# The last expert's down products, scatter and sums moved into the gMLP block, with its down weights loaded by rows in two parts

## The reference

```python
def _expert_choice_ffn(x, norm_g, w_router, w_e_gate, w_e_up, w_e_down):
    ...
    gate, idx = lax.top_k(jnp.swapaxes(aff, 1, 2), cap)
    xg = xn[bidx, idx]
    h = (jax.nn.silu(jnp.einsum('becd,edf->becf', xg, w_e_gate))
         * jnp.einsum('becd,edf->becf', xg, w_e_up))
    yo = jnp.einsum('becf,efd->becd', h, w_e_down) * gate[..., None].astype(xg.dtype)
    return jnp.zeros((B, S, D), yo.dtype).at[bidx, idx].add(yo)

def gmlp_mixer(h, w_in, v_gain, w_sp, b_sp, w_out):
    uv = jax.nn.gelu(h @ w_in)
    u, v = jnp.split(uv, 2, axis=-1)
    v = layer_norm_gain(v, v_gain)
    ...
    return (u * z.reshape(B, S, D_GATE)) @ w_out
```

## Time and profile before

| | us |
|---|---|
| three runs | 1567.84, 1568.64, 1570.01 (median 1568.64) |
| the profiled execution | 1567.67 |
| its span, first to last instruction | 1565.6 |
| PE busy | 1333.9 (85%) |
| PE weight loads busy | 846.7 (54%) |
| DVE, ACT, POOL busy | 513.4, 483.1, 221.9 |
| mean granted TensorE clock | 0.942 of full |

### The profile page before, as it was taken

How to read it: one execution, slowest core, us unless ns; L and a number is a source line. 1 busy time by engine, 2 the same in 40 slices (tenths; PEclk the granted TensorE clock), 3 DMA queues, 4 the chain that set the end, 5 groups by cost and what they waited for, 6 DMA issues and landing times. The chain is left out here.

```text
span 1565.6 us, 18070 instructions
## 1 busy us (share of the span) xinstructions
PE 1333.9 (85%) x7114; PEld 846.7 (54%) x7114; DVE 513.4 (33%) x874; ACT 483.1 (31%) x739; POOL 221.9 (14%) x134
## 2 busy tenths in 40 slices
PE   7999999998766676766767677899999999999998
PEld 7778878633221221121212122777888777778886
DVE  5887768310000000000000000544333436643333
ACT  6656664310000000000000000635444367564442
POOL 0010000000000000000000000662232171123221
PEclk9999999999989988779998987999999999999999
DMA  7564437999999999999999999655556464365650
GB/s 243 173 173 116 119 126 285 391 428 428 430 430 430 430 429 430 430 430 430 430 429 430 429 430 422 238 161 182 189 171 204 142 200 138 99 198 178 197 165 27
DMA packets 123296, 446.81 MB, mean 285 GB/s; under 512 B 9193, under 2 KB 61801, under 8 KB 98673
## 3 DMA queue, kind: packets, MB, share of 16 engines
q1 hardware_dynamic: 121616, 445.30, 73.7%
q10 hardware_dynamic: 1632, 0.88, 0.2%
HBM read 445.10 MB, written 1.05 MB: 285 GB/s over the span
## 5 line engine op out<-in xcount | busy, mean ns | idle before, releaser
L1459 PE MATMUL ps<-sb_ring,sb_consts 128*32 128x384 f32 x2032 | 204.0, 539 | 120.0 <-DMA sb_ring<-w_e_up 98.0
L1459 PEld LDWEIGHTS ps<-sb_ring,sb_consts 128*32 128x32 f32 x2032 | 61.5, 116 | 260.2 <-DMA sb_ring<-w_e_up 144.4
L169 PE MATMUL ps<-net_whi,sb_xhi 128*128 128x512 f32 x480 | 190.0, 396 | 5.1 <-DVE sb_xlo L242 3.3
L1480 PE MATMUL ps<-sb_e_ring,sb_hT 128*32 128x512 f32 x576 | 191.9, 649 | 2.1 <-DMA sb_e_ring<-w_e_down 1.9
L171 PE MATMUL ps<-net_whi,sb_xlo 128*128 128x512 f32 x480 | 187.1, 390 | 0.0
L170 PE MATMUL ps<-net_wlo,sb_xhi 128*128 128x512 f32 x480 | 186.9, 389 | 0.0
L1480 PE MATMUL ps<-sb_ring,sb_hT 128*32 128x512 f32 x192 | 114.2, 758 | 54.4 <-DMA sb_e_ring<-w_e_down 53.6
L1871 ACT ACTIVATE net_whi<-sb_ring 128x2048 fp32r<-128x2048 f32 x64 | 122.3, 1914 | 64.0 <-PE ps L171 61.7
L1559 DVE TENSOR_TENSOR sb_sg<-ps,sb_sg 128x384 f32<-128x384 f32 x16 | 8.9, 557 | 365.3 <-PE ps L1459 365.3
L1884 POOL TENSOR_TENSOR net_wlo<-sb_ring,net_whi 128x2048 fp32r<-128x2048 f32 x20 | 92.2, 4610 | 215.3 <-ACT net_whi L1871 215.3
L1884 DVE TENSOR_TENSOR net_wlo<-sb_ring,net_whi 128x2048 fp32r<-128x2048 f32 x44 | 101.0, 2295 | 51.0 <-ACT net_whi L1871 51.0
(11 more groups left out here) (355 smaller groups left out, 1902.3 us busy)
## 6 DMA issues: line engine op xcount, KB each, us to landing
sb_ring<-w_e_up SPq DMA_DIRECT2D x64, 1536.0 KB, 37.7
sb_ring<-w_e_gate SPq DMA_DIRECT2D x63, 1536.0 KB, 37.0
sb_e_ring<-w_e_down SPq DMA_DIRECT2D x48, 1536.0 KB, 35.3
sb_ring<-ffn_w_gu SPq DMA_DIRECT2D x88, 512.0 KB, 4.6
sb_ring<-w_e_down SPq DMA_DIRECT2D x16, 1536.0 KB, 32.5
sb_ring<-ffn_w_down SPq DMA_DIRECT2D x22, 1024.0 KB, 4.9
sb_ring<-w_in SPq DMA_DIRECT2D x40, 512.0 KB, 3.6
sb_ring<-a_w_in SPq DMA_DIRECT2D x8, 1024.0 KB, 13.4
```

What stands on the lines that cost most here:

```text
L169: pe.matmul(out, hi, whi, start=start, stop=False)
L1459: mm = pe.matmul(ps[j * CAP:(j + 1) * CAP, GATE if i < 4 else UP, 0:FJ], xgs[:, k, :], rows[:, q * E_FF + j * FJ:q * E_FF + (j + 1) * FJ], ...
L1480: mm = pe.matmul(ps[j * CAP:(j + 1) * CAP, DOWN[h], :], hT[:, b, j * CAP:(j + 1) * CAP], expert_unit(m, NGU + j)[:, b * D + h * BANK:b * D ...
```

## The change

- The last expert leaves the loops. Its hidden part stays in the experts' block on PE, ACT and DVE. The transposes, the copy of `hT`, down products, scatter and the copies to `m.x` stand at the start of the gMLP block, the copies between the splits of the first granules.
- Its down weights come in two parts (`load_last_rows`): of each partition's three rows of 4 KB the first two, for all four groups, then the third. The products go by the same parts, all four groups side by side. Ahead of the first part PE does six 128x512 products whose result nothing reads, ahead of the second one.
- v0 is cut into four granules of two chunks (128 x 1024, half a MB) for two of four. The six granules that SP issues ahead are now v0 and v1.
- x is turned and split in halves of four chunks, each once its half of x is copied.
- Buffers that must outlive the experts' block move: two units form `m.mid`, which the mixer's stream and the attention use too, and `e_ring`, `hotgs`, `sg`, `hT` lie on the right side of the memory; gMLP's `ut`, `vt`, `tmp`, `wsp` and `gain` take expert units.

```diff
+def load_last_rows(sp, m, I, e, i):
+
+    b0, nb = ((0, FB - 1), (FB - 1, 1))[i]
+    src = I["w_e_down"][0, e, :, :].rearrange("(j p b) n -> p j (b n)", b=FB, p=P)[:, :, b0 * D:(b0 + nb) * D]
+    sp.dma_start(expert_unit(m, NGU)[:, b0 * D:(b0 + nb) * D], src[:, 0, :]).then_inc(m.e_landed[NGU + i], 16)
+    dst = m.e_ring[:, 0:3 * SLOT].rearrange("p (j n) -> p j n", j=3)[:, :, b0 * D:(b0 + nb) * D]
+    sp.dma_start(dst, src[:, 1:, :]).then_inc(m.e_landed[NGU + i], 16)
...
-            with sp.Fori(2, N_EXP) as e:
+            with sp.Fori(2, LAST) as e:
                 for i in range(NS):
                     load(e, i)
+            for i in range(NGU):
+                load(LAST, i)
+            sp.wait_ge(used, LAST * NS)
+            for i in range(2):
+                load_last_rows(sp, m, I, LAST, i)
             sp.wait_ge(used, (N_EXP - 1) * NS + RING)
             for g in range(st.slots):
                 st.load(sp, g)
...
-    for name, n0 in (("v0", D), ("v1", D + BANK), ("u0", 0), ("u1", BANK)):
+    at["v0"] = [st.add([(0, 2, BANK, chunks(I["a_w_in_2"][0], k, 2, D, BANK))], True) for k in range(0, DC, 2)]
+    for name, n0 in (("v1", D + BANK), ("u0", 0), ("u1", BANK)):
...
+            act.wait_ge(g_ps, 1)
+            act.activation(m.gs, ps[:, UP, 0:SEQ], ACT.Copy).then_inc(gs_ready, 1)
+            act.wait_ge(y_ps, 1)
+            act.activation(m.ysb[:, 0:BANK], ps[:, DOWN[0], :], ACT.Copy).then_inc(y_act, 1)
             st.split_hi(act, first)
-            norm_hi_act(act, m, use, NB, m.xhi, col(m, "gmlp"), xhi_ready, 0)
-            st.split_hi(act, first + 1)
+            for h in range(2):
+                act.wait_ge(sum_ps, T * h + 1)
+                act.activation(m.x[:, 0, h * BANK:(h + 1) * BANK], ps[:, h, :], ACT.Copy).then_inc(x_act, 1)
+                if h == 0:
+                    st.split_hi(act, first + 1)
+            norm_hi_act(act, m, use, NB, m.xhi, col(m, "gmlp"), xhi_ready, 0, range(4))
+            st.split_hi(act, first + 2)
+            norm_hi_act(act, m, use, NB, m.xhi, col(m, "gmlp"), xhi_ready, 0, range(4, DC))
+            st.split_hi(act, first + 3)
...
-            turn_tokens(pe, m, m.x, NB)
+            for b in range(FB):
+                mm = pe.transpose(ps[:, GATE, b * P:(b + 1) * P], m.sg[:, :].rearrange("c (p b) -> c b p", b=FB)[:, b, :], m.ident)
+            mm.then_inc(hT_ps, 1)
+            for t in range(T):
+                mm = pe.transpose(ps[:, UP, t * P:(t + 1) * P], m.hotgs[:, t, :, :].rearrange("p j c -> p (j c)"), m.ident)
+            mm.then_inc(g_ps, 1)
+            pe.wait_ge(hT_ready, 1)
+            for i, (rows, idle) in enumerate((((0, 1), 6), ((2,), 1))):
+                for _ in range(idle):
+                    pe.matmul(ps[:, GATE, :], m.ident, m.x[:, 0, 0:BANK], start=True, stop=True)
+                pe.wait_ge(m.e_landed[NGU + i], (LAST + 1) * 32)
+                for h in range(2):
+                    for b in rows:
+                        for j in range(J):
+                            mm = pe.matmul(ps[j * CAP:(j + 1) * CAP, DOWN[h], :], m.hT[:, b, j * CAP:(j + 1) * CAP],
+                                           expert_unit(m, NGU + j)[:, b * D + h * BANK:b * D + (h + 1) * BANK],
+                                           start=b == 0, stop=b == FB - 1)
+                    if i == 1:
+                        mm.then_inc(y_ps, 1)
+            pe.wait_ge(gs_ready, 1)
+            for h in range(2):
+                pe.wait_ge((y_act, y_dve)[h], 1)
+                for t in range(T):
+                    pe.matmul(ps[:, 2 * t + h, :], m.gs[:, t * P:(t + 1) * P], m.ysb[:, h * BANK:(h + 1) * BANK],
+                              start=False, stop=True, skip_group_check=True).then_inc(sum_ps, 1)
+            for h in range(2):
+                pe.wait_ge(x_act, h + 1)
+                pe.wait_ge(x_dve, h + 1)
+                for c in range(4 * h, 4 * h + 4):
+                    for t in range(T):
+                        mm = pe.transpose(turned_ps(m, NB, c)[:, t * P:(t + 1) * P], m.x[:, t, c * P:(c + 1) * P], m.ident)
...
+            dve.wait_ge(hT_ps, 1)
+            dve.tensor_copy(m.hT[:, :, :].rearrange("p b c -> p (b c)"), ps[:, GATE, 0:FJ]).then_inc(hT_ready, 1)
+            dve.wait_ge(y_ps, 2)
+            dve.tensor_copy(m.ysb[:, BANK:], ps[:, DOWN[1], :]).then_inc(y_dve, 1)
             st.split_lo(dve, first)
-            norm_lo_dve(dve, m, use, NB, m.xhi, m.xlo, col(m, "gmlp"), xhi_ready, xlo_ready, 0)
-            for i in range(1, 4):
-                st.split_lo(dve, first + i)
+            for h in range(2):
+                dve.wait_ge(sum_ps, T * h + 2)
+                dve.tensor_copy(m.x[:, 1, h * BANK:(h + 1) * BANK], ps[:, 2 + h, :]).then_inc(x_dve, 1)
+            for g, some in ((1, range(4)), (2, range(4, DC))):
+                norm_lo_dve(dve, m, use, NB, m.xhi, m.xlo, col(m, "gmlp"), xhi_ready, xlo_ready, 0, some)
+                st.split_lo(dve, first + g)
+            for g in range(3, 6):
+                st.split_lo(dve, first + g)
```

More of the change, by code:

```diff
@@ L13 @@
+import math
 from contextlib import ExitStack
@@ L1265 @@
 SLOT = GK * E_FF
-RING, RING2 = 4, 5
+RING, RING2, MID = 4, 3, 2
 NGU = 8
@@ L1316, in experts @@
         GATE, UP, DOWN = 4, 5, (6, 7)
[L1318 removed]
+        LAST = N_EXP - 1
         xgT = sb("xgT", [P, DC, N_EXP * CAP])
@@ L1410, in _ @@
                 act.activation(xgT[:, c, CAP:], ps[:, DOWN[n % 2], CAP:], ACT.Copy, scale=gain[:, c:c + 1]).then_inc(xg_act, 1)
-            with act.Fori(1, N_EXP) as e:
+            with act.Fori(1, LAST) as e:
                 hidden(e)
                 out(e)
-            for h in range(2):
-                act.wait_ge(scattered, 2 * (N_EXP - 1) + h + 1)
-                act.activation(m.x[:, 0, h * BANK:(h + 1) * BANK], ps[:, ACC[h], :], ACT.Copy)
+            hidden(LAST)
         @block.tensor
@@ L1505, in _ @@
             out(1)
-            with pe.Fori(2, N_EXP) as e:
+            with pe.Fori(2, LAST) as e:
                 hidden(e)
                 out(e)
+            hidden(LAST)
         @block.vector
@@ L1572, in _ @@
                 dve.tensor_scalar(xgT[:, c, CAP:], ps[:, DOWN[n % 2], CAP:], gain[:, c:c + 1], None, ALU.mult).then_inc(xg_dve, 1)
-            with dve.Fori(1, N_EXP) as e:
+            with dve.Fori(1, LAST) as e:
                 hidden(e)
                 out(e)
-            for h in range(2):
-                dve.wait_ge(scattered, 2 * (N_EXP - 1) + h + 1)
-                dve.tensor_copy(m.x[:, 1, h * BANK:(h + 1) * BANK], ps[:, ACC[2 + h], :])
+            hidden(LAST)
         @block.gpsimd
@@ L1757, in _ @@
                 for j, g in enumerate(at[name]):
+                    if i == 0:
+                        dense_granule(pe, st, g, [ps[:, b, :] for b in zb(i)], m.xhi, m.xlo, 2 * j, BANK, j == 0, j == 3,
+                                      (xlo_ready, range(1, DC + 1)))
+                        continue
                     for part in ((0, 2), (2, 4)):
@@ L1761, in _ @@
                         dense_granule(pe, st, g, [ps[:, b, :] for b in zb(i)], m.xhi, m.xlo, 4 * j, BANK, j == 0, j == 1,
-                                      (xlo_ready, range(1, DC + 1)) if i == 0 else None, part)
+                                      None, part)
                     if name == "u1" and j == 0:
@@ L2424, in program, with room @@
         m.e_landed = [sem(f"e_landed{i}") for i in range(NS)]
+        m.mid = sb("mid", [P, MID * SLOT])
         st, at = second_stream(m, ctx, nc, I)
-        with ExitStack() as first:
-            m.ring2 = first.enter_context(nc.sbuf_tensor("sb_ring2", [P, RING2 * SLOT], F32))
-            mixer(nc, m, I)
-            experts(nc, m, I, st)
-        m.xhi, m.xlo = sb("xhi2", [P, DC, SEQ], F32R), sb("xlo2", [P, DC, SEQ], F32R)
-        st.place_halves(ctx, nc, "net")
-        m.zero = sb("zero", [P, BANK], F32R)
-        gmlp(nc, m, I, st, at, 2)
+        with ExitStack() as late:
+            def room(name, *shape):
+                return late.enter_context(nc.sbuf_tensor("sb_" + name, [P, *shape], F32, side="right"))
+            with ExitStack() as first:
+                m.ring2 = first.enter_context(nc.sbuf_tensor("sb_ring2", [P, RING2 * SLOT], F32))
+                mixer(nc, m, I)
+                m.spare = first.enter_context(nc.sbuf_tensor("sb_spare", [P, SLOT], F32))
+                m.e_ring = room("e_ring", (SPARE - RING - RING2 - MID) * SLOT)
+                m.hotgs, m.sg, m.hT = room("hotgs", T, P // CAP, CAP), room("sg", FJ), room("hT", FB, P)
+                a = CONSTS["anti"][0]
+                m.gs, m.ysb = m.consts[:, a:a + SEQ], m.xs[:, 1, :]
+                experts(nc, m, I, st)
+            m.xhi, m.xlo = sb("xhi2", [P, DC, SEQ], F32R), sb("xlo2", [P, DC, SEQ], F32R)
+            st.place_halves(ctx, nc, "net")
+            m.zero = sb("zero", [P, BANK], F32R)
+            gmlp(nc, m, I, st, at, 2)
         swiglu(nc, m, I, st, at, 0, 3)
```

67 lines of the change are left out of this document (45 added, 22 removed).

## The result

The changed kernel takes **1572.80 us** (median of 11 runs, 1571.12 to 1574.99) against 1568.44 us for the kernel before on the same chip (11 runs, 1567.17 to 1571.92). The ratio is 1.0029 with a 95% interval of 1.0019 to 1.0038: slower by 4.4 us. The profiled execution has a span of 1571.0 us, where the one of before had 1565.6. The forecast was 1572.4 us.

What follows compares the result with a forecast made beforehand. Weight loading bounds the expert loop, PE the stretch after the seam. First gMLP product 4.6 us later, less 0.8 for the gap, gives 3.8 on the median 1568.64: 1572.4 us, range 1568.5 to 1575.5.

Steps and rivals of the forecast that it cites:

- The barrier: After the last expert's hidden part: PE, ACT and DVE wait for SP's last issue, going on at 969.4.
- Rival 1: At the barrier after the hidden part: SP does not hold it; 6.0 us earlier, 1561.8 us; chance 0.13.
- idle products: Ahead of the down products: six, then one, wholly on the path, 14 steps of 0.43 us, 6.0 us.
- clock: After PE's idle time, from 969.4: low clock into the idle products, loss 0.8 to 2.4 us, taken as 1.5.
- down products: Last expert's, four groups at once: 8 steps, 3.4 us, then 4 steps, 1.7 us; end at 983.6.
- scatter and turn: Between down products and first gMLP product: scatter 3.7 us, turn and splits 1.8 us; first product at 989.1.
- The gap in v0: PE's 0.76 us wait for a 2048-wide low part in v0 goes with half-size granules, saving 0.8 us.
- at nothing: In the seam: w_spT and the gain, issued earlier with 10 us more to land, cost nothing.
- Rival 2: At the barrier: SP holds it less, or the clock rises at once; 1569 to 1571 us; chance 0.20 with Rival 4.
- Rival 3: Clock low through all idle products and the first down part: 4 to 5 us for 1.5; 1576 us; chance 0.05.
- Rival 4: Behind the seam: a later wait takes up the late start, at most 3.8 us, 1568.6; chance 0.20 with Rival 2.

Runs made afterwards that it cites:

- e4: The kernel before with only v0 in four half-MB granules and x's high and low parts interleaved with their splits: 1565.88 us, ratio 0.9990 to before.
- e1: The changed kernel with all six gMLP loads issued behind the barrier instead of ahead of it: 1563.56 us, ratio 0.9958 to the kernel before.
- e2: The changed kernel with four gMLP loads (v0) ahead of the barrier and two (v1) behind it: 1570.29 us, one run.
- e3: The changed kernel without its seven idle products, the loads still ahead of the barrier: 1566.75 us, ratio 0.9987 to the kernel before.
- e6: As e1 but without any idle product: 1561.49 us, ratio 0.9954 to the kernel before.
- e7: As e5 but with down weights and products by groups, two and two, and no idle product ahead of the second half: 1564.00 us, ratio 0.9971 to before.
- e5: As e1 but with three idle products ahead of the first down part instead of six: 1560.89 us, ratio 0.9951 to the kernel before.
- e8: As e5 but with POOL's masking of w_spT behind the norm's POOL part: 1561.97 us, ratio 0.9959 to the kernel before.

## Why the prediction was right, point by point

**The barrier: right, and shown.** The step on which the forecast stood was that SP must issue its last load before PE, ACT and DVE may go on, at 969.1. It ended at 969.18. From U, 4 MB of gMLP's loads were issued by + 14.08 before (four loads), + 14.12 after and + 14.00 in e4 (six loads each): here the nearest row by bytes was the right one. e1 takes SP's issues away and the 13.1 us wait becomes 1.0; e2 takes two of six away and the barrier follows. Rival 1, that SP does not hold it, was wrong as a description of the change, and right as a price: it had 6.0 us earlier at the first product than before, and e1, in which SP doesn't hold it, is 5.84 us earlier (29.43 to 23.59). Its 1561.8 us is missed by 1.8, of which 0.67 is the gap that it took as gone. In the change PE left the barrier 0.44 us after SP, where the prediction had 0.3, and had been idle since 956.56 instead of 958.5; neither changes the sum by more than 0.2 us.

The Trainium skill, DMA: Bandwidth & Descriptors, section "Issuing engines are not separate DMA queues", calls the sequencer's time to start a DMA usually small beside the transfer. The trace after disagrees for a queue that is backed up: one issue of half a MB took 15.13 us, and an all-engine barrier paid for it.

**What the hold is worth.** With no idle products on either side, e3 against e6, the first gMLP product is 29.20 - 23.39 = 5.8 us later with the hold. That is less than the 12 us by which the barrier itself moves (from U + 2.6 to + 14.6), since without the hold PE must wait for weights until U + 10 anyway. The idle products behind the hold cost another 6.35 (after against e3). Together 12.2, against 11.96 between after and e1, where six of them overrun a little as well. The loss of 4.4 us therefore needs both: e3 keeps the hold, leaves out only the idle products, and has its first gMLP product 0.2 us before that of the kernel before and a ratio of 0.9987.

**The terms that were mis-sized.** The prediction's *idle products* and *clock* came to 6.0 + 1.5 = 7.5 us. Measured: 971.16 to 978.45 and 982.02 to 983.08, 7.29 + 1.06 = 8.35. Of the 0.85 too little, 0.6 is the clock (2.1 us for 1.5; it rose 5.5 us after PE resumed, where the prediction allowed 3.1 to 6.2), and 0.2 that the single idle product costs 1.06 rather than 0.86 (it stands between products of another tile shape, which may be why; no run separates it). The *down products* took 3.57 and 1.87 us for the 3.4 and 1.7 of the text, and the *barrier* let PE go 0.2 us later. These add up to the end of the down products at 984.95 for 983.6. The *scatter and turn* took 5.66 us for 5.5. So the first product came at 990.61, not 989.1: 6.1 us late, not 4.6.

**The gap in v0: the right number from a wrong cause.** It went, 0.8 us as forecast (tail 580.4 for 581.2). The prediction put the gap down to the width of the granule, and the work of w_spT "at nothing" for its landing alone. The kernel before shows another cause, POOL's masking of w_spT:

```profile
986.35 2.41 POOL L1728 TENSOR_TENSOR sb_wsp<-sb_wsp,sb_consts 128x1024 f32<-128x1024 f32 x1 [71.63 <-DMA sb_wsp<-w_spT]
986.98 8.54 DVE L157 TENSOR_TENSOR net_wlo<-sb_ring,net_whi 128x2048 fp32r<-128x2048 f32 x3
```

The first of these three low parts took 3.93 us, from 986.98 to 990.91, the other two 2.29 each. At 2.29 it would have ended at 989.27, and PE began to wait only at 990.20. So 2048-wide parts were in time, and what made the gap was the masking, 0.63 us ahead of the low part. The half-size granules alone did not remove it: in e1, e4, e6 and e7, all with half-size granules, the masking fell on a low part and cost PE 0.67 to 1.41 us. In the change the landing was so late, and the seam too, that POOL masked at 981.45, when DVE was idle.

**The number.** The two profiled executions differ by 5.4 us, 6.1 less 0.8; the forecast had 3.8. The medians differ by 4.4. The forecast of 1572.4, made from 3.8 above the median of the runs shown, is 0.4 from the measured 1572.8. That nearness is partly luck: at the first product the sum was 1.5 us short, and the interval of the ratio (3.0 to 6.0 us) holds 3.8 and 5.4 alike, so the time cannot tell them apart. Rivals 2, 3 and 4 did not occur: SP's last issue was not earlier, the clock was not low throughout, and nothing behind took up the late start. Rival 3 was also priced too low: 20 steps at 0.86 for 0.43 us lose 8.6 us, not 4 to 5, which puts it near 1579.5 and not 1576.

**Where the change's gain went.** Taken one by one the parts do gain: small granules 2.0 us at the first product (e4), rows instead of groups 3.2 (e7 against e5). Without the hold the whole is 5.8 better than before (e1), 7.0 with three idle products (e5). With it, 12.0 are given back, for a net of 6.1 worse.

## What to carry to other kernels

Before work is moved behind an all-engine barrier, find which queue will arrive last and what it still has to issue: look-ahead loads behind a backed-up DMA queue held SP here until 0.8 us before the last of the expert's weights landed (969.18 and 969.99), and belong behind the barrier when the barrier's other side has work waiting. Products that only keep PE's clock up are free only inside a wait that the trace shows; count them against that wait (here three), and take them out where something else has used it up. And before a gap is put down to the size of the operation that ends late, compare that operation's time with its twins: here 3.93 us stood beside 2.29, and the cause was on another engine.

## What the runs showed of the hardware that was not expected

**The time of one issue does not follow its own bytes.** Between 962 and 969 us, with the last of the expert's weights still to land (969.99), an issue of half a MB held SP for 2.26 us and one of 1 MB for 2.45 and 2.33 (after). So halving v0's loads did not halve their issue time, though 4 MB in all were issued by the same point from U as before. What it is in the queue that fills up (transfers, rows or bytes) was not separated by any run.

**VectorE and GpSimd hold each other up for whole instructions.** A 128x1024 low part takes 1.2 us alone, 3.41 when POOL's masking began 0.08 us before it (e4) and 3.00 when it began 0.48 us before (e7). The other way round, DVE's two low parts beginning 0.22 us ahead keep their 2.35 us, and POOL's 2.4 us operation takes 4.40 (e5): it ends 987.11 - 984.84 = 2.3 us after DVE is through. In each case the engine that started second ends about one own duration after the other's end (1.08, 1.08 and 2.27 us). They do not alternate: in e5 POOL waited for both of DVE's low parts, the second of which began later than POOL's operation. The low parts of x, which take one input from PSUM, were not held up: in e1 four took 1.66 us, as in the change, with the masking beginning 0.74 us into them. This is what the Trainium skill says in SBUF — State Buffer, section "SBUF: two separate sides": the port pair that the two engines share is an exclusive lock, held for the whole instruction by whichever starts first, where the VectorE operation has two SBUF inputs and the GpSimd operation reads SBUF. Both hold for the low parts and the masking. The traces agree on the whole instruction, and the prediction should have used it.

**The clock at the same point differs between executions.** With the barrier free, the transposes of the last expert ran at the low clock in e1, e6 and e8 (0.88 us for three) and at the high one in e5 and e7 (0.58 and 0.59 us). The programs of e5 and e8 differ only in where POOL masks w_spT, more than 20 us later. A price for the clock can therefore be given for a stretch only as a range, and one profiled execution shows one value of it.
